# Context behind the tokens in the opening of a hybrid GLA trunk layer on one core

## The reference

```
mods(v)  = silu(v) @ w_mod + b_mod                 # shift and scale: first 2 of 6 blocks of 1024 columns
h        = rmsnorm(x,   w) * (1 + scale)  + shift  # 1024 tokens, v = c
hc       = rmsnorm(ctx, w) * (1 + cscale) + cshift # 256 rows,    v = c_ctx
proj     = h @ w_in                                # queries, keys, values, gate, convolution, pooling
pc       = hc @ w_in[:, keys..gate]
...                                                # gated linear attention, convolution, pooling, w_out
out      = final rmsnorm of (x + g1 * mix + g2 * MLP)
```

## Time and profile before

| | us |
|---|---|
| median of three runs (lowest, highest) | 1088.19 (1086.53, 1090.26) |
| profiled execution | 1089.87 |
| its span | 1088.0 |
| TensorE busy in the span | 1062.0 |
| V1 begins, from the span's start | 67.84 |

### The profile page before, as it was taken

One profiled execution on the slowest core, in us unless ns is written; L12 is line 12 of the kernel. 1 busy time (PEld: TensorE's weight loads), 2 busy tenths in 40 slices (PEclk: granted clock), 3 DMA queues, 4 the chain that ended last, 5 costly groups with the idle time before them and its releaser, 6 DMA issues.

```text
span 1088.0 us, 16279 instructions
## 1 busy us (share of the span) xinstructions
PE 1062.0 (98%) x5512; PEld 851.8 (78%) x5512; DVE 826.6 (76%) x1070; ACT 508.9 (47%) x818; POOL 307.9 (28%) x280
## 2 busy tenths in 40 slices
PE   8999999999999999998999999999999999999995
PEld 4578888777778888787888888888778888888884
DVE  4887869737544987799878787787987777777776
ACT  5657533356624312576666666666422222222234
POOL 1000006287301344013232323323333122222322
PEclk9999999999999999999999999999999999999998
DMA  9523240011013555225857566667746844864604
GB/s 369 225 97 116 89 142 31 31 40 40 21 40 136 231 191 216 78 78 227 315 229 273 232 257 245 239 262 284 295 168 259 334 185 184 339 253 185 256 1 155
DMA packets 58900, 199.80 MB, mean 184 GB/s; under 512 B 5600, under 2 KB 6880, under 8 KB 58336
## 3 DMA queue, kind: packets, MB, share of 16 engines
q1 hardware_dynamic: 58848, 199.11, 48.3%
HBM read 139.32 MB, written 59.77 MB: 183 GB/s over the span
## 4 chain that ended last, share of the span: by engine, by line
PE 49%; DVE 4%; issue 1%; POOL 0%; DVEq 0%; ACT 0%; ACTq 0%; POOLq 0%
PE ob L1382 13%; PE main L1424 13%; PE sm L1382 10%; PE sm L1424 8%; PE ob L1424 5%; DVE XR L2632 1%; DVE XR L2699 1%; DVE slot L2463 1%; DVE stage L2513 1%; DVE slot L2458 0%; DVE stage_last L2513 0%; DVE t_tmp L2497 0%; DVE t_tmp L2506 0%; DVE hid L2520 0%; DVE hid L2499 0%
## 5 line engine op out<-in xcount | busy, mean ns | idle before, releaser
L953 PE MATMUL main<-a_hi,w_hi 128*128 128x512 f32 x376 | 125.8, 416 | 0.0
L1382 PE MATMUL ob<-h_sum,slot 128*128 128x512 f32 x504 | 122.8, 393 | 3.0 <-DVE hid L2520 3.0
L1838 ACT ACTIVATE slot<-raw 128x512 fp32r<-128x512 f32 x80 | 50.2, 631 | 153.1 <-PE main L1424 58.4
L953 PE MATMUL main<-a_lo,w_hi 128*128 128x512 f32 x376 | 116.7, 391 | 0.0
L953 PE MATMUL main<-a_hi,w_lo 128*128 128x512 f32 x376 | 116.2, 390 | 0.0
L1382 PEld LDWEIGHTS ob<-h_sum,slot 128*128 128x128 f32 x504 | 95.7, 190 | 23.4 <-issue 3.4
L2632 DVE SCALAR_TENSOR_TENSOR XR<-main,mods,XR 128x512 f32<-128x512 f32 x112 | 83.3, 748 | 28.8 <-PE main L1424 27.7
L953 PEld LDWEIGHTS main<-a_hi,w_lo 128*128 128x128 f32 x376 | 70.6, 188 | 15.6
L953 PEld LDWEIGHTS main<-a_lo,w_hi 128*128 128x128 f32 x376 | 70.6, 188 | 15.6
L953 PEld LDWEIGHTS main<-a_hi,w_hi 128*128 128x128 f32 x376 | 66.7, 188 | 17.9 <-issue 5.8
L1424 PE MATMUL main<-t_even,slot 128*128 128x512 f32 x336 | 78.1, 389 | 0.0
(11 more groups left out here) (354 smaller groups left out, 2453.7 us busy)
## 6 DMA issues: line engine op xcount, KB each, us to landing
hidden_kept<-stage SPq DMA_DIRECT2D x98, 512.0 KB, 4.2
raw<-wstream SPq DMA_DIRECT2D x60, 512.0 KB, 4.3
...
```

Of the source, the lines that this page charges most:

```text
L953: ins = pe.matmul(main[:, bank, half * HALF:(half + 1) * HALF], w[:, slot, k, :], x[:, half * HALF:(half + 1) * HALF], start=begin, stop=end)
L1382: ins = pe.matmul(hid_bank(acc, odd), slots1[j][:, w, kp, :], parts[x][:, kp, :], start=PARTS[j][3] and kp == 0 and m == 0, stop=kp == KP ...
L1838: act.activation(slots2[j][:, 0, :, :, :], operand(s, j), ACT.Copy).then_inc(w2_hi, 1)
```

## The change

It touches the opening alone, up to V1.

- SP loads the tokens first; the context comes behind the fourth of eight modulation pieces. A piece now has 256 columns and is read in rows of 1 KB. Each waits for the square of the block with the same number, with which it shares a semaphore.
- The filler shrinks from 18 to 10 products. ACT squares the tokens alone. DVE adds two pairs of squares; TensorE sums six squares of 1024 columns, the last one half by half.
- The modulation is made block by block: eight rows of 256 columns in four column groups, eight turns, eight copies (the first by DVE, the others by ACT) and eight pairs of DVE instructions.
- The loop over k handles tokens alone, in the order `modulation(k)`, `scale1(k)`, `low1(k)` on DVE for k = 1 to 7, with the context's work put in between from k = 2 on: squares (ACT), their sums (DVE, TensorE), root (ACT), scaling (DVE).
- On TensorE each k has its turn, gate, value and rows in this order; the context's 40 products follow behind the tokens of the last block. The gate's token result is copied out on its own, and the split of the second tile stands behind that on ACT and DVE.

```diff
-GROUPS = 3
+GROUPS = 4
 ROWS = 32 * GROUPS
...
+FILL = (10, 2)
...
-SMALL = [(_name, _j) for _j in range(KT // 2) for _name in ("rows", "turn")]
+SMALL = [(_name, _j) for _j in range(KT) for _name in ("rows", "turn")]
...
-        wmod = [at(f"wmod{j}", [P, KT, HALF], F32, HA + place * KIB) for j, place in enumerate((0, 32, 16, 48))]
+        wmod = [at(f"wmod{j}", [P, KT, 2 * P], F32, HA + (j % 2 * 32 + j // 2 * 8) * KIB) for j in range(KT)]
...
+        squares1 = at("squares1", [P, 6, N], F32, ZA + 8 * KIB)
+        squares1_late = at("squares1_late", [P, 2, N], F32, ZT)
+        squares_c = at("squares_c", [P, KT, NC], F32, ZT + 8 * KIB)
...
             def load_wmod(j):
-                sp.dma_start(wmod[j][:, :, :].rearrange("p k c -> p (k c)"), wm1[j]).then_inc(wmod_loaded[j], 16)
+                sp.wait_ge(sq1_made, j + 1)
+                sp.dma_start(wmod[j][:, :, :], wm1[j // 2].rearrange("p (k j c) -> p k j c", j=2, c=2 * P)[:, :, j % 2, :]
+                             ).then_inc(x_wmod_loaded[j], 16)
...
-            sp.dma_start(xs[:, :, N:NA], ct).then_inc(ctx_loaded, 16)
             for k in range(KT):
-                sp.dma_start(xs[:, k, 0:N], xt[k]).then_inc(x_loaded[k], 16)
+                sp.dma_start(xs[:, k, 0:N], xt[k]).then_inc(x_wmod_loaded[k], 16)
             load_wmod(0)
             sp.dma_start(wg[:, :, :].rearrange("p k c -> p (k c)"), wg_in).then_inc(wg_loaded, 16)
+            load_wmod(1)
             load_tile(0)
-            load_wmod(1)
             load_wmod(2)
             load_wmod(3)
+            sp.dma_start(xs[:, :, N:NA], ct).then_inc(ctx_loaded, 16)
+            load_wmod(4)
+            load_wmod(5)
             sp.dma_start(gw[:, :, :].rearrange("r h c -> r (h c)"), gw_in).then_inc(gw_loaded, 16)
+            load_wmod(6)
+            load_wmod(7)
             sp.dma_start(small[:, NFIRST:NSMALL], small_in[:, NFIRST:NSMALL]).then_inc(masks_loaded, 16)
             for t in range(1, 4):
                 load_tile(t)
             sp.wait_ge(h1_lo, KT)
+            sp.wait_ge(c1_lo, KT)
...
                     g = k % GROUPS
-                    ins = pe.matmul(sm[32 * g:32 * g + 32, s % 2, :], silu_wide[:, k, :], wmod[j][:, k, :],
+                    ins = pe.matmul(sm[32 * g:32 * g + 32, s % 2, 0:2 * P], silu_wide[:, k, :], wmod[j][:, k, :],
...
-                for q in range(4):
+                for q in range(2):
...
+            for ready, k in (((sq1_made, 1), 0), ((sq1_made, 2), 1), ((acc1_made, 1), 2), ((acc1_made, 2), 4), ((sq1_made, 7), 6)):
+                pe.wait_ge(*ready)
+                sums_of(square_place(k), (1, 0), k == 0, False)
+            for n, half in enumerate((1, 0)):
+                pe.wait_ge(sq1_made, KT + n)
+                sums_of(square_place(7), (half,), False, True).then_inc(sums1_done, 1)
             modulation_rows(0)
             modulation_turned(0)
             modulation_rows(1)
-            modulation_turned(1)
...
+            def token_products(k, m, rows, w, x, first=False, last=False):
+                for half in range(2):
+                    ins = pe.matmul(main[rows, m, half * HALF:(half + 1) * HALF], w, x[:, k, half * HALF:(half + 1) * HALF],
+                                    start=first and k == 0, stop=last and k == KT - 1)
...
+            def context_products(k, m, rows, w, c, first=False, last=False):
+                return pe.matmul(ob[rows, m * HALF:m * HALF + NC], w, c[:, k, :], start=first and k == 0, stop=last and k == KT - 1)
+
+            wide, narrow = slice(0, 4 * RANK), slice(0, 2 * RANK)
+
+            def gate_high(k, last=False):
+                pe.wait_ge(h1_hi, k + 1)
+                return token_products(k, 0, wide, wg_parts[:, k, :], a_hi, first=True, last=last)
+
+            def gate_low(k):
                 pe.wait_ge(h1_lo, k + 1)
...
+                token_products(k, 0, narrow, wg_parts[:, k, 0:2 * RANK], a_lo)
+
+            def value_high(k):
+                if k == 0:
+                    pe.wait_ge(hi_made, 1)
+                token_products(k, 1, slice(0, P), w_hi[:, 0, k, :], a_hi, first=True)
+                token_products(k, 1, slice(0, P), w_hi[:, 0, k, :], a_lo)
+
+            def value_low(k):
                 if k == 0:
                     pe.wait_ge(split_done, 1)
...
+                token_products(k, 1, slice(0, P), w_lo[:, 0, k, :], a_hi, last=True)
...
-            gate_part(0)
-            value_part(0)
+            gate_high(0)
+            modulation_turned(1)
+            gate_low(0)
+            value_high(0)
             modulation_rows(2)
...
+            value_low(0)
+            for k in range(1, KT - 1):
+                modulation_turned(k + 1)
+                gate_high(k)
+                gate_low(k)
+                value_high(k)
+                if k + 2 < KT:
+                    modulation_rows(k + 2)
+                value_low(k)
+                if k == 3:
+                    pe.wait_ge(squares_c_added, 2)
+                    for q in range(2):
+                        ins = pe.matmul(ob[:, HALF:HALF + NC], ones, squares_c[:, q, :], start=q == 0, stop=q == 1)
+                    ins.then_inc(sums_c_done, 1)
+            gate_low(KT - 1)
+            gate_high(KT - 1, last=True).then_inc(sums1_done, 1)
+            value_high(KT - 1)
+            value_low(KT - 1)
+
+            for k in range(KT):
+                pe.wait_ge(c1_hi, 2 * k + 1)
+                if k < KT - 1:
+                    context_products(k, 0, wide, wg_parts[:, k, :], c_hi, first=True)
+                pe.wait_ge(c1_lo, k + 1)
+                context_products(k, 0, narrow, wg_parts[:, k, 0:2 * RANK], c_lo)
+            context_products(KT - 1, 0, wide, wg_parts[:, KT - 1, :], c_hi, last=True).then_inc(tile_done, 1)
+            for k in range(KT):
+                context_products(k, 1, slice(0, P), w_hi[:, 0, k, :], c_hi, first=True)
+                context_products(k, 1, slice(0, P), w_hi[:, 0, k, :], c_lo)
+                ins = context_products(k, 1, slice(0, P), w_lo[:, 0, k, :], c_hi, last=True)
+            ins.then_inc(tile_done, 1)
...
+            def root1(cols):
+
+                act.activation(rs1[:, cols], rs1[:, cols], ACT.Exp, scale=-0.5).then_inc(rs1_made, 1)
+
+            for k in range(KT):
+                act.wait_ge(x_wmod_loaded[k], 16)
+                if k < KT - 1:
+                    act.activation(square_place(k), xs[:, k, 0:N], ACT.Square).then_inc(sq1_made, 1)
+                else:
+                    for half in (1, 0):
+                        cols = slice(half * HALF, (half + 1) * HALF)
+                        act.activation(square_place(k)[:, cols], xs[:, k, cols], ACT.Square).then_inc(sq1_made, 1)
+
+            for n, half in enumerate((1, 0)):
+                cols = slice(half * HALF, (half + 1) * HALF)
+                act.wait_ge(sums1_done, n + 1)
+                log1(cols, main[:, 1, cols])
+                act.wait_ge(rs1_made, 2 * n + 1)
+                root1(cols)
...
+            def context_high(k):
+                act.wait_ge(c1_scaled, k // 4 + 1)
+                act.activation(c_hi[:, k, :], xs[:, k, N:NA], ACT.Identity, bias=ab1[:, k, 1:2],
+                               scale=ab1[:, k, 3:4]).then_inc(c1_hi, 1)
+                act.activation(xs[:, k, N:NA], xs[:, k, N:NA], ACT.Identity, bias=ab1[:, k, 1:2],
+                               scale=ab1[:, k, 3:4]).then_inc(c1_hi, 1)
+
...
+                act.wait_ge(*ab_ready(k))
...
+                    for half in (1, 0):
+                        cols = slice(half * HALF, (half + 1) * HALF)
+                        act.wait_ge(x_scaled, 2 - half)
+                        ins = act.activation(a_hi[:, k, cols], xs[:, k, cols], ACT.Identity, bias=ab1[:, k, 0:1],
+                                             scale=ab1[:, k, 2:3])
+                    ins.then_inc(h1_hi, 1)
...
+                    act.wait_ge(x_scaled, k + 3)
+                    act.activation(a_hi[:, k, :], xs[:, k, 0:N], ACT.Identity, bias=ab1[:, k, 0:1]).then_inc(h1_hi, 1)
+                if k + 1 < KT:
+                    copy_rows(k + 1)
+                if k == 0:
+                    weight_high(0)
+                elif k == 2:
+                    act.wait_ge(ctx_loaded, 16)
+                    act.activation(squares_c[:, :, :], xs[:, :, N:NA], ACT.Square).then_inc(squares_c_made, 1)
+                elif k == 4:
                     act.wait_ge(gw_loaded, 16)
                     act.activation(gw_parts[0:64, :, :], gw[0:64, :, :], ACT.Copy)
                     act.activation(gw_parts[96:128, :, :], gw[96:128, :, :], ACT.Copy)
                     act.activation(gw_hi[64:96, :, :], gw[64:96, :, :], ACT.Copy).then_inc(gw_rounded, 1)
-
+                    act.wait_ge(sums_c_done, 1)
+                    log1(slice(N, NA), ob[:, HALF:HALF + NC])
+                    act.wait_ge(rs1_made, 5)
+                    root1(slice(N, NA))
+                elif k >= 5:
```

(85 more changed lines are left out.)

192 lines of the change are left out of this document (25 added, 167 removed).

## The result

| | before | after |
|---|---|---|
| median, 20 runs each (us) | 1088.10 (1086.04 to 1090.92) | 1091.44 (1090.17 to 1094.85) |
| ratio after to before | | 1.0031 [1.0024, 1.0038] |
| profiled execution, its span | 1089.87, 1088.0 | 1093.76, 1091.9 |
| V1 begins | 67.84 | 69.99 |
| V2 (the tile behind V1) begins | 83.91 | 87.00 |

The forecast was 1086.4 in a range from 1083.8 to 1090.0. The kernel became 3.3 us slower, so the range missed it and the sign was wrong. The trace shows the same: V1 begins 2.15 us later instead of 1.8 earlier, and between V1 and V2 another 0.94 us is lost. V3 keeps that distance (2.98 us later, at 103.11 against 100.13); at the end of the span it is 3.9.

The account below looks back on a forecast made before the run. It took TensorE and DVE, both nearly full in the opening, as the bound. V1 at 65.0 instead of 67.84 gave 2.8 us, less 1.0 for the clock: 1.8 off the median 1088.19, so 1086.4, range 1083.8 to 1090.0.

Parts of the forecast that it names:

- the clock's term: Opening, TensorE: two falls of the granted clock, each costing nothing to 1.33 us, taken as 0.5 each, 1.0 together.
- Sums and first product: Start of the opening: last sum of squares ends at 21.5 instead of 24.7 us, low part of block 0 at 28.3.
- rival 3: Loop: TensorE bounds it as row sets save less, steps 4.3 to 4.75 us; 1090.3 at most; chance 0.07.
- The loop: Blocks 1 to 7: seven DVE and ACT steps of 4.1 us plus 0.3, low part of block 7 ends at 57.3.
- The tail: From block 7's low part to V1: context work on ACT, then the second tile's split comes last, V1 at 65.0.
- Rival 2: Behind V1: `mbuf` issued late behind the fourth tile's load delays DVE; all gain lost, 1088.2; chance 0.12.
- Rivals 4 and 5: Opening: short packets make the last modulation piece late, 1096, chance 0.05; loop waits keep the clock at 0.50, 1112, chance 0.06.

Follow-up runs that it names:

- clock_and_mods: Changed kernel with idle products in the first-stage pauses and ahead of the last block's low part, and two `mbuf` loads before the fourth tile's: 1087.63 us, ratio 1.0000.
- before_fill: Kernel before the change with five idle products in its own opening pauses, nothing else: 1088.97 us, ratio 1.0005 to the kernel before.
- clock_first: Changed kernel with idle products in the two TensorE pauses of the first stage: 1090.19 us, ratio 1.0021 to the kernel before.
- clock_tail: Changed kernel with three idle products ahead of the last block's low part: 1090.05 us, ratio 1.0022 to the kernel before.
- mods_first: Changed kernel with the two first `mbuf` loads issued ahead of the fourth tile's load: 1089.80 us, ratio 1.0022 to the kernel before.
- rows_and_sums: clock_and_mods with DVE one block ahead, row sets, first tile's split and gate weights' copies moved earlier, six idle products instead of ten: 1088.98 us, ratio 1.0006.

## Why the prediction was wrong

The marks of its sum, with V1 as it stood without the clock's term:

| | forecast | after | clock_and_mods |
|---|---|---|---|
| last sum ends | 21.5 | 21.7 | 22.2 |
| low part of block 0 ends | 28.3 | 28.5 | 29.0 |
| low part of block 7 ends | 57.3 | 60.6 | 58.9 |
| V1 | 65.0 | 70.0 | 66.8 |

- **Sums and first product**: right within 0.2 us. From the last sum to the low part of block 0 all three columns have 6.8 us; in clock_and_mods all marks lie 0.5 us later, since the same filler took 8.85 instead of 7.90 us. The row sets are 1.07 us where 1.0 was worked out, so rival 3 fell.
- **The loop**: 29.0 forecast, 29.9 with the clock up (clock_and_mods), 32.1 in the changed kernel. A step is 4.2 instead of 4.1 us, and one is 4.6: the two products of the context's sum, 1.02 us on TensorE, stand ahead of a turn there and had been left out. That is a term short by 0.9.
- **The tail**: 7.7 forecast, 7.9 with the clock up, 9.4 in the changed kernel. That the split of the second tile would be last was wrong in the changed kernel, where it ended at 68.7, 1.3 us ahead of V1. With the clock up it ended at 66.6, 0.15 us ahead: there it and TensorE are level.
- **The clock, the step that failed.** It took 1.0 us, with 2.7 as the bound. The columns differ by 2.2 us in the loop and by 1.5 in the tail, 3.7 us, in one execution each. The prediction had foreseen where the clock would fall (near 26 and near 58; it fell at 27 and at 61) but expected one or two microseconds at 0.50, where the first fall alone had six. It priced a fall by the one row set that it had seen slowed, 1.33 us, as the upper bound, and took 0.5 because TensorE would have some slack. The price is not that of the one instruction that stood there: while the clock is 0.50 products take up to nearly twice as long (1.05 instead of 0.61 us, 1.94 instead of 1.07), and a stretch of 6 us full of products holds 3 us less by estimate. In the kernel before, the low stretch held little more than that row set; in the changed kernel it held a whole block's products, and DVE waits for the turns behind them. The slack, too, was assumed without a row: even in the kernel before DVE waited for the slowed row set (before_fill).
- **Rival 2** had a chance of 0.12 and came true beside the forecast, not instead of it: `mbuf` late behind the fourth tile's load, 0.94 us. The argument against it, that DVE waits 2.33 us for ACT there, was too weak: the loads were issued at 69.16 instead of 63.32, 5.8 us later, more than the 2.33 could take.
- **Together**, in the profiled execution: 65.0 + 0.2 + 0.9 + 0.2 + 3.7 is V1 at 70.0, 4.0 later than the forecast's 66.0, and with the 0.9 behind V1 the end should come 4.9 late. It was forecast for this execution at 1088.1 and took 1093.76, 5.7 more, so 0.8 us arose behind V2. The profiled execution lies 2.3 us above the median of its kernel. At the median the miss is 5.0 us, of which the ratios of clock_first and clock_tail give the falls 2.1 (1.1 more than assumed) and that of mods_first gives the loads 1.0; the sums, the loop and the tail add 1.3. The remaining 1.6 us stay open. One step of the prediction fits them by size: it took its gain from V1 at 67.84, an execution with a fall worth some 1.33 us ahead of V1, and then subtracted it from the median of all executions, 1.7 us lower. No run shows how many of those have that fall.
- **Rivals 4 and 5**: the short packets were slower than the row they were priced by, 348 instead of 386 GB/s, and hidden all the same; a wait for them shows only in rows_and_sums. The loop did not hold the clock down: from 36 to 60 us it was 1.00, with 1.5 us of pauses in 24. The Trainium skill's rule that was weighed there (TensorE: Matmul & The Clock Gate, HAM oscillation — how this bites in real kernels) does not describe this loop. The next section of that page, A second HAM failure mode: psum-queue depth-cycling, comes nearer to the first stage: it tells of a kernel whose short idle times between groups of products, often repeated, make the clock swing between its two levels. The trace agrees only as far as that short pauses, 1.88 and 1.14 us with little work between them, preceded a fall; it shows no swing. The prediction's reading that the trace of the kernel before has one fall was incomplete: there is another at 512 us, far from the change (last section).
